# Two regroupings of small TensorE matmuls: the norms of the recurrence's keys, and the context tokens of 16 experts

## The reference, cut to what matters

```
kk = k * k_k                                  # 8 heads x 64 channels, all 1280 tokens
kk = kk / sqrt(max(sum over the head's 64 channels of kk*kk, 1e-24))
gate = sigmoid(hg) @ gate_g2                  # 96 -> 512, latent tokens
```

```
hid = silu(xs @ w_gate[e]) * (xs @ w_up[e])   # 1024 -> 512
y   = (hid @ w_down[e]) * g                   # 512 -> 1024, added to the tokens' rows
```

## Time and profile before

| what | us |
|---|---|
| median of 3 runs | 4953.11 |
| the profiled execution, its own time | 4949.38 |
| its span, first to last instruction | 4947.5 |
| stage `keys`, first instruction to last multiplication's start (and the two in that group 1.02) | 750.14 to 791.46 |
| stage `l_experts`, first expert's first matmul to the last L3765 record | 3384.88 to 3845.2 |
| TensorE busy over the span | 4450.3 |

### The profile page before, as it was taken

One profiled execution on the slowest core, in us unless ns is written; L12 is line 12 of the kernel. 1 busy time (PEld: TensorE's weight loads), 2 busy tenths in 40 slices (PEclk: granted clock), 3 DMA queues, 4 the chain that ended last, 5 costly groups with the idle time before them and its releaser, 6 DMA issues. The chain is left out here.

```text
span 4947.5 us, 88138 instructions
## 1 busy us (share of the span) xinstructions
PE 4450.3 (90%) x38558; PEld 3460.5 (70%) x38558; DVE 2129.5 (43%) x3034; ACT 1365.6 (28%) x2025; POOL 1069.1 (22%) x756
## 2 busy tenths in 40 slices
PE   6999996999998989999979899987999688997897
PEld 3878885899994568888858567764555574775776
DVE  2026544444443233422431244436655413444886
ACT  2114202222221110000022223223555212322674
POOL 2310122444432123333321010011211111000211
PEclk9998997999998989999979889998999798998998
DMA  7310100000007211111131100047887210003998
GB/s 278 98 49 1 48 22 27 4 4 4 4 4 304 93 34 51 47 47 51 47 102 26 43 5 1 24 169 263 272 274 225 84 38 22 1 22 111 325 375 286
DMA packets 322590, 480.24 MB, mean 97 GB/s; under 512 B 43665, under 2 KB 201322, under 8 KB 313042
## 3 DMA queue, kind: packets, MB, share of 16 engines
q1 hardware_dynamic: 301778, 399.61, 23.5%
q0 software_dynamic: 17024, 63.11, 4.6%
q10 hardware_dynamic: 3456, 12.58, 0.7%
HBM read 420.71 MB, written 54.53 MB: 96 GB/s over the span
## 5 line engine op out<-in xcount | busy, mean ns | idle before, releaser
L3871 DVE TENSOR_TENSOR l_experts_lo<-l_raw_room,l_experts_hi 128x1024 fp32r<-128x1024 f32 x256 | 300.5, 1222 | 64.3 <-ACT l_experts_hi L3807 64.1
L3807 ACT ACTIVATE l_experts_hi<-l_raw_room 128x1024 fp32r<-128x1024 f32 x256 | 256.3, 1059 | 69.3 <-PEq L69 34.0
L180 PE MATMUL mlp_ps<-h_hi,mlp_w_hi 128*128 128x512 f32 x512 | 200.6, 392 | 6.1 <-DVE h_lo L565 6.1
L180 PE MATMUL mlp_ps<-h_lo,mlp_w_hi 128*128 128x512 f32 x512 | 200.0, 391 | 0.0
L180 PE MATMUL mlp_ps<-h_hi,mlp_w_lo 128*128 128x512 f32 x512 | 199.9, 390 | 0.0
L1767 POOL TENSOR_TENSOR rec_lv<-rec_ab,rec_masks 128x512 f32<-128x512 f32 x120 | 145.0, 1225 | 243.6 <-DVE rec_ab L1684 157.2
L1703 DVE TENSOR_TENSOR rec_x<-rec_x,rec_all_ps 128x1024 f32<-128x1024 f32 (+1 forms) x100 | 111.4, 1114 | 194.0 <-PE rec_all_ps L1485 194.0
L2351 ACT ACTIVATE mlp_hid_hi<-mlp_pos 128x1024 f32 x32 | 34.0, 1062 | 569.3 <-DVE mlp_pos L2365 569.3
L155 POOL CAST mlp_w_hi<-mlp_w 128x1024 fp32r<-128x1024 f32 x64 | 68.4, 1069 | 501.7 <-issue 228.2
L180 PE MATMUL mlp_ps<-mlp_hid_hi,mlp_w_hi 128*128 128x512 f32 x448 | 174.3, 389 | 0.0
L180 PE MATMUL mlp_ps<-mlp_hid_lo,mlp_w_hi 128*128 128x512 f32 x448 | 174.3, 389 | 0.0
(11 more groups left out here) (734 smaller groups left out, 11605.3 us busy)
## 6 DMA issues: line engine op xcount, KB each, us to landing
l_raw_room<-in_w_gate_dram SPq DMA_DIRECT2D x128, 512.0 KB, 5.8
l_raw_room<-in_w_up_dram SPq DMA_DIRECT2D x128, 512.0 KB, 7.4
l_experts_raw_down<-in_w_down_dram SPq DMA_DIRECT2D x64, 1024.0 KB, 5.1
rec_out_w_ada<-in_w_ada_dram SPq DMA_DIRECT2D x24, 1024.0 KB, 12.2
mlp_w<-in_w_mlp_up_dram SPq DMA_DIRECT2D x32, 512.0 KB, 3.9
mlp_w<-in_w_mlp_down_dram SPq DMA_DIRECT2D x32, 512.0 KB, 3.6
l_choose_w_ada<-in_w_ada_dram POOLq DMA_DIRECT2D x16, 1024.0 KB, 16.8
l_in_w<-in_w_in_dram SPq DMA_DIRECT2D x18, 512.0 KB, 4.1
```

Of the source, the lines that this page charges most:

```text
L180: mm = self.nc.tensor.matmul(ps[0:rows, c, 0:n], w[b][:, k, 0:rows], x[:, k, t0:t0 + n], start=(k + j == 0), stop=(k == kt - 1 and j == 2))
L3807: nc.scalar.activation(hi[:, q % RING], piece(e, u), ACT.Copy).then_inc(hi_done, 1)
L3871: nc.vector.tensor_tensor(lo[:, q % RING], piece(e, u), hi[:, q % RING].bitcast(F32), ALU.subtract).then_inc(lo_done, 1)
```

## The change

In `prepare_recurrence`: the sums put the squares in the moving operand and `pick` (a 32-column window of a 66-column table) in the weights, on 4 column tiles, each a quarter of the unit's tokens, all units accumulating into one 128 x 128 area. The spreading uses 4 row tiles of 32 with 128-column weights from a new table `couples`, each into its own bank; `bc` has two sets of four banks. Gate tiles 0 and 1 are made after unit 2 of the sums, tiles 2 and 3 right after the sums, their copies behind squares 5 and 8 and behind the root. `gout` has four buffers. The first set but one of the spreading waits for all gate copies.

In `run_experts` with `NG == 2`: the context products are taken out of the per-piece loop and run after 4 up pieces (twice per expert) and after 2 down pieces (twice). `used` is raised after the six latent matmuls. SP waits for the new semaphores `few_up` and `few_down`, as do `gate` and `outputs`.

```diff
-        ss, bc, pg = s.ps("ss", [P, 4 * TT, 2]), s.ps("bc", [P, 3, 512]), s.ps("pg", [P, 2, 2, 512])
+        bank = s.ps("bank", [P, 8, 512])
+        ss, pg = bank[:, 7, 0:P], bank[:, 0:4].rearrange("p (a c) t -> p a c t", a=2)
+        bc = bank[:, ::-1].rearrange("p (a c) t -> p a c t", a=2)
...
+                    if q in (5, 8):
+                        copy_gate(q // 3 - 1)
                 act.wait_ge(clamped, 1)
                 nc.scalar.activation(rs[:], rs[:], ACT.Sqrt).then_inc(rooted, 1)
+                copy_gate(2)
+                copy_gate(3)
...
-                    for c in range(n // P):
-                        mm = nc.tensor.matmul(ss[:, first[q] + c], sq[:, q % 3, c * P:(c + 1) * P], pick[:],
-                                              start=True, stop=True)
+                    for c in QUARTERS:
+                        mm = nc.tensor.matmul(ss[32 * c:32 * c + 32, 0:w], pick[:, 32 - 2 * q:64 - 2 * q],
+                                              sq[:, q % 3, c * w:(c + 1) * w], start=(q == 0), stop=(q == N - 1),
+                                              tile_position=(0, 32 * c))
                     mm.then_inc(summed, 1)
+                    if q == 2:
+                        pe.wait_ge(loaded, 32)
+                        pe.wait_ge(g_ready, 1)
+                        gate(0)
+                        gate(1)
+                gate(2)
+                gate(3)
+                pe.wait_ge(coupled, 4)
                 pe.wait_ge(inv_done, 1)
...
+                    if q == 1:
+                        pe.wait_ge(g_copied, 4)
+                    if q >= 2:
+                        pe.wait_ge(keys_done, q - 1)
+                    for c in QUARTERS:
+                        rows = slice(32 * c, 32 * c + 32)
+                        mm = nc.tensor.matmul(bc[:, q % 2, c, 0:w], couples[rows, q], rs[rows, 0:w], start=True,
+                                              stop=True)
                     mm.then_inc(spread, 1)
...
+                for c in QUARTERS:
+                    rows = slice(32 * c, 32 * c + 32)
+                    nc.vector.tensor_copy(couples[rows].rearrange("p a (h i) -> p (a h) i", h=2),
+                                          ident[rows, 32 * c:32 * c + 2 * N].unsqueeze(2).to_broadcast([32, 2 * N, 64])
+                                          ).then_inc(coupled, 1)
```

```diff
+    FEW_UP, FEW_DOWN = KT // 2, FT // 2
...
-                        sp.wait_ge(used if NG == 2 else lo_done, place[e - 1, 2 * c + 1] + 1)
+                    if e and NG == 1:
+                        sp.wait_ge(lo_done, place[e - 1, 2 * c + 1] + 1)
+                    elif e and c < UP // 2:
+                        sp.wait_ge(few_up, UP // FEW_UP * (e - 1) + 2 * c // FEW_UP + 1)
+                    elif e:
+                        sp.wait_ge(few_down, FT // FEW_DOWN * (e - 1) + (2 * c - UP) // FEW_DOWN + 1)
...
-                        for j in range(4 if NG == 2 else 0):
+                        mm.then_inc(used, 1)
+                        if NG == 2 and k % FEW_UP == FEW_UP - 1:
+                            few_hidden(e, range(k + 1 - FEW_UP, k + 1))
+
+                def few_hidden(e, ks):
+                    for k in ks:
+                        for j in range(4):
                             mm = nc.tensor.matmul(
                                 pC[32 * j:32 * j + 32, 0:2 * P].rearrange("p (a f) -> p a f", a=2), x_few[:, k],
                                 piece(e, k).rearrange("p (a f) -> p a f", a=2)[:, :, j * P:(j + 1) * P],
                                 start=(k == 0), stop=(k == UP - 1), tile_position=(0, 32 * j))
-                        mm.then_inc(used, 1)
+                    mm.then_inc(few_up, 1)
```

More of the change, by code:

```diff
@@ L1277, in prepare_recurrence @@
     units = [(m, t0, n) for m in range(4) for t0, n in CHUNKS]
-    TT = T // P
-    first = [m * TT + t0 // P for m, t0, _ in units]
+    N = len(units)
+    QUARTERS = range(4)
+    assert units[0][2] == 512 and 2 * N <= 32
     with Stage(nc, name) as s:
         kvec, g2 = s.sb("kvec", [P, 4]), s.sb("g2", [96, 512])
-        pick = s.sb("pick", [P, 2])
-        sq, rs = s.sb("sq", [P, 3, 512]), s.sb("rs", [P, 4 * TT, 2])
-        hg, gout = s.sb("hg", [96, L]), s.sb("gout", [P, 2, L])
-        ss, bc, pg = s.ps("ss", [P, 4 * TT, 2]), s.ps("bc", [P, 3, 512]), s.ps("pg", [P, 2, 2, 512])
+        pick, couples = s.sb("pick", [P, 66]), s.sb("couples", [P, N, P])
+        sq, rs = s.sb("sq", [P, 3, 512]), s.sb("rs", [P, P])
+        hg, gout = s.sb("hg", [96, L]), s.sb("gout", [P, 4, L])
+        bank = s.ps("bank", [P, 8, 512])
+        ss, pg = bank[:, 7, 0:P], bank[:, 0:4].rearrange("p (a c) t -> p a c t", a=2)
+        bc = bank[:, ::-1].rearrange("p (a c) t -> p a c t", a=2)
         loaded, scaled, squared, summed, picked = (s.sem("loaded"), s.sem("scaled"), s.sem("squared"),
                                                    s.sem("summed"), s.sem("picked"))
+        cleared, coupled = s.sem("cleared"), s.sem("coupled")
         clamped, rooted, inv_done, spread, keys_done = (s.sem("clamped"), s.sem("rooted"), s.sem("inv"),
@@ L1299, in _ @@
                     sp.wait_ge(g_copied, m + 1)
-                    sp.dma_start(g_dram[m * P:(m + 1) * P, :], gout[:, m % 2]).then_inc(g_stored[m % 2], 16)
-                for b in range(2):
-                    sp.wait_ge(g_stored[b], 32)
+                    sp.dma_start(g_dram[m * P:(m + 1) * P, :], gout[:, m]).then_inc(g_stored, 16)
+                sp.wait_ge(g_stored, 64)
             @block.scalar
@@ L1308, in _, with copy_gate @@
                 nc.scalar.activation(lora_in[0:32, :], lora_a[0:32, :], ACT.Tanh)
+                def copy_gate(m):
+                    act.wait_ge(g_done, m + 1)
+                    nc.scalar.activation(gout[:, m], pg[:, m % 2].rearrange("p c t -> p (c t)"), ACT.Copy
+                                         ).then_inc(g_copied, 1)
                 for q, (m, t0, n) in enumerate(units):
@@ L1339, in _ @@
                     mm.then_inc(summed, 1)
[L1340 to L1343, removed]
-                pe.wait_ge(inv_done, 1)
[L1345 to L1352, removed]
+                    if q == 2:
[3 more added lines that the diff above has]
+                        gate(1)
@@ new lines, in _ @@
+                gate(2)
+                gate(3)
+                pe.wait_ge(coupled, 4)
+                pe.wait_ge(inv_done, 1)
+                for q, (_, _, n) in enumerate(units):
+                    w = n // 4
+                    if q == 1:
[6 more added lines that the diff above has]
+                                              stop=True)
@@ L1353, in _ @@
                     mm.then_inc(spread, 1)
-                    if q in (3, 6):
-                        gate(q // 3 + 1)
             @block.vector
             def _(dve):
+                nc.vector.memset(pick[:], 0.0).then_inc(cleared, 1)
+                dve.wait_ge(cleared, 1)
                 for j in range(2):
-                    nc.vector.memset(pick[64 * j:64 * j + 64, 1 - j:2 - j], 0.0)
-                    last = nc.vector.memset(pick[64 * j:64 * j + 64, j:j + 1], 1.0)
+                    last = nc.vector.memset(pick[64 * j:64 * j + 64, 32 + j:33 + j], 1.0)
@@ L1368, in _ @@
                 nc.vector.memset(lora_in[64:65, :], 1.0)
-                dve.wait_ge(summed, len(units))
-                nc.vector.tensor_scalar(rs[:], ss[:], 1e-24, None, ALU.max).then_inc(clamped, 1)
+                for c in QUARTERS:
[3 more added lines that the diff above has]
+                                          ).then_inc(coupled, 1)
+                dve.wait_ge(summed, N)
+                nc.vector.tensor_scalar(rs[:], ss, 1e-24, None, ALU.max).then_inc(clamped, 1)
                 dve.wait_ge(rooted, 1)
@@ L1374, in _ @@
                     dve.wait_ge(spread, q + 1)
-                    nc.vector.tensor_tensor(kk[:, m, t0:t0 + n], kk[:, m, t0:t0 + n], bc[:, q % 3, 0:n], ALU.mult
-                                            ).then_inc(keys_done, 1)
+                    own = kk[:, m, t0:t0 + n].rearrange("p (c t) -> p c t", c=4)
+                    nc.vector.tensor_tensor(own, own, bc[:, q % 2, :, 0:n // 4], ALU.mult).then_inc(keys_done, 1)
 class Order:
@@ L3653, in run_experts @@
         y_read, passed = s.sem("y_read"), s.sem("passed")
+        few_up, few_down = s.sem("few_up"), s.sem("few_down")
         def piece(e, u):
@@ L3763, in down, with few_out @@
                                                       **flags)
-                        for j in range(4 if NG == 2 else 0):
+                        mm.then_inc(used, 1)
+                        if NG == 2 and f % FEW_DOWN == FEW_DOWN - 1:
+                            few_out(e, range(f + 1 - FEW_DOWN, f + 1))
+                def few_out(e, fs):
+                    for f in fs:
+                        for j in range(4):
                             mm = nc.tensor.matmul(pZ[32 * j:32 * j + 32, 0:256], h_few[:, e % 2, f],
```

(7 more changed lines are left out.)

6 lines of the change are left out of this document (3 added, 3 removed).

## The result

The changed kernel takes 4888.52 us (median of 4 runs, 4881.68 to 4898.37) against 4949.79 (median of 4); ratio 0.9878, 95% interval 0.9866 to 0.9891. That is 61 us less, where 55.5 were forecast, and inside the range. The profiled execution is the slowest of the four, 4898.37 with a span of 4896.6.

What follows compares the result with a forecast made beforehand. TensorE was taken to set the pace in the experts and in `keys` up to the spreading. Savings of 43.5 us (experts) and 12 us (keys), together 55.5, off a 4953.1 median gave 4897 us; 8-in-10 range 4884 to 4915.

Steps and rivals of the forecast that it cites:

- TensorE sets the pace in both stages: In the experts TensorE is busy for all 28.11 us of a step; in `keys` it sets the pace up to the spreading.
- A context group in a run costs 0.43 us: Experts: a piece's context products need two 256-column passes, 0.43 us inside a run against 0.77 to 0.81 alone.
- A group removed saves 0.34 us: Experts: each context group no longer alone saves 0.34 us; 8 removed per expert, 43.5 us over 16 experts.
- The upper bound, built on the last layer's row: Experts: six latent matmuls at the last layer's 1.36 us leave 0.81 per lone group, so 0.38 us saved, 49 in all.
- No new wait shows: Experts: the new semaphore waits of ScalarE and SP were costed at nothing, covered by ScalarE's 9.9 us free per step.
- the walk's slack: Experts: following one step's times, the first up pair freed at 7.6 us has 15.5 us to load.
- the 14.0 of the earlier trace: Experts: a load was said to land within 14.0 us even in the last layer, where DMA is full.
- Keys: 12 us: In `keys` the last multiplication was to end at 780.5 instead of 792.5, 12 us saved, range 7 to 14.
- the forecast's lower bound of 7 us: In `keys`, everything at the lower clock: the last multiplication ends at 785.3, saving 7 us.
- Loads in the open: Experts: weight loads stand between a run's passes, a group removed saves 0.12 us, part 15 us, total 4926; chance 0.05.
- DMA as the bound: Experts: DMA fills at share 0.90, step 26.5 us, part 25 us, total 4916; chance 0.09.
- Late up buffers: Experts: up loads taking 20 us stall TensorE, step 29.9 us, total 4970, slower than before; chance 0.02.

Runs made afterwards that it cites:

- e1: The experts' part alone, with `prepare_recurrence` from the kernel before; ratio 0.9904 to the kernel before, step 25.18 us, expert stage 416.7 us.
- e8: The changed kernel with each context run doing only its last piece, so context work is left out; steady step 21.69 us.
- e5: The changed kernel with all 8 up pieces' context products in one run; step 24.2 to 27.1 us, mean 25.48, expert stage 423.7 us.
- e7: The changed kernel with all 8 up and all 4 down pieces in one run each; mean step 25.37 us, ratio 0.9899 to the kernel before.
- e2: The keys' part alone, with `run_experts` from the kernel before; ratio 0.9978 to the kernel before, `keys` 31.13 us.
- e3: The changed kernel with context products after each single piece again, 12 runs per expert; step 28.11 us, `keys` 34.57 us.
- e12: The changed kernel with all 4 down pieces' context products in one run, timed; 4884.2 us, ratio 0.9868 to the kernel before.
- e9: The changed kernel with all four gate tiles in `keys` made behind the sums; `keys` 27.83 us, total 4893.85 us.

## Why the prediction was right

- *TensorE sets the pace in both stages, so each microsecond saved there comes off.* Right for the experts: it is busy for all of every step before and after, and e1 turned 2.93 x 16 = 46.9 us of steps into a stage 45.7 shorter. In `keys` the stage as a whole bears it out, but no run changed TensorE's work there alone.
- *A context group in a run costs 0.43 us.* Right: 0.436 (e8).
- *A group removed saves 0.34 us, bounds 0.31 to 0.38.* Mis-sized: (28.107 - 25.180) / 8 = 0.366. I took 0.2325 us as what a latent matmul costs in this stage. It costs 0.227 in long stretches (1.36 / 6), here as in the last layer; the slower spacing is itself a trace of the group before it. The upper bound, built on the last layer's row, had it. The step is 25.18 for 25.4, and the stage 45.7 us shorter for 43.5. By the traces the two parts beat the forecast by 2.7 us; the other 3 of the 6 in the medians are within their scatter, as 0.9866 to 0.9891 is 12 us wide.
- *No new wait shows.* Right for TensorE, with the walk's slack: the loads into the up buffers land in 5.4 and 6.9 us (medians) against 15.5 allowed. The walk read the 14.0 of the earlier trace rows as a bound, but it is a median of seven, so half of those loads took at least as long; the slack was larger than that error. Runs e5 and e7 show the same loads turning into a wait once buffers are freed at 15.3 us and all together.
- *Keys: 12 us.* 12.5 in the profiled pair. By the walk's steps, less the 2.98 us of later start: gates 0 and 1 end at 762.3 as forecast, sums at 766.9 (767.5), the spreading starts at 770.5 (772.7, since gates 2 and 3 ran at the full clock), the last multiplication ends at 780.0 (780.5). The sum came out in part by luck: the start was 2.2 us early, and the spreading took 9.5 us for 7.8 and gave 1.7 of that back. The lower clock, in that trace from 777.3 on, explains only part of this: the spreading lasted 9.1 us in e2, with 5.5 us of it at the full clock against 3.8 here, and 9.8 in e3, with 2.5. The forecast was short on the turns between TensorE and VectorE: VectorE is idle for 0.2 to 0.5 us before seven of the twelve multiplications. Ten traces of this code give 29.8 to 31.1 us but for one of 34.6, so the forecast's lower bound of 7 us was a real case.
- *Rivals.* Loads in the open would have shown a step of 27.2: fell. DMA as the bound: fell, and its premise with it (e8). Late up buffers: the mechanism exists (e5, e7), at a lower price than I gave it there, and the change stays on the near side of it.

## What to carry to other kernels

Count how often TensorE goes over to the small column-tiled float32 matmuls and back, not only the matmuls: each run cost 0.35 to 0.42 us here, nearly as much as the 8 small records themselves. Group them until the buffers that they hold become late, and read that limit from the time between a buffer's release and its next use, since the gain turns over within one size (4 up pieces per run gained, 8 lost). Look at the whole stage and not at the steady step alone: a buffer released late is paid for at the end (e12). A busy share of DMA near 1 is no proof of a bound; an engine on the critical path that waits for a DMA is.

## What the hardware showed that I had not expected

- After a context run the latent matmuls stay slow beyond the first: pieces of 1.51 and 1.38 us, then 1.36, in the rows above. This goes with 12 runs to 6 giving 0.35 us per run and 6 to 4, which first left long stretches, 0.42. The same slow start follows float32 transposes on the full array in the last layer. What in the array or its queue keeps them slow, no run here shows.
- DMA moved 350 GB/s at a share of 1.05 without one wait of TensorE in that step, where 271 GB/s at 0.85 and 310 at 1.00 had looked nearly full.
- Four column tiles at a time, 128 columns each, were enough for the granted clock to rise to its full level, before any dense matmul of 512 columns had run in that stage (e9); the old sums, 80 records of 2 columns, ran 17 us at the lower one.
